# Expert loop of a hybrid decoder trunk: the down product of one expert moved behind the gate and up products of the next

## The reference

```python
def hier_moe(h, ...):            # top-1 of 4 groups, then top-2 of its 8 experts
    ...
    for e in range(N_EXPERTS):   # 32
        y = (jax.nn.silu(t @ w_gate[e]) * (t @ w_up[e])) @ w_down[e]
        out = out + combine[:, e:e + 1] * y
```

## Time and profile before

| | |
|---|---|
| median of 3 runs | 908.18 us (905.06 to 909.02) |
| the profiled execution | 908.32 us, its span 906.6 us |
| TensorE matmul busy | 829.3 us, 91% of the span |
| TensorE weight load busy | 573.5 us, 63% |
| VectorE / ScalarE / GpSimd busy | 331.0 / 200.2 / 153.5 us |
| moved by DMA | 265.19 MB |

### The profile page before, as it was taken

The page is one execution under the profiler, slowest core; times in us unless marked ns, Lnnn a source line. Parts: engine busy times, 40 slices in busy tenths (PEclk is TensorE's granted clock), DMA queues, the critical chain, the costliest instruction groups (busy, mean ns, idle before and its releaser), DMA issues.

```text
span 906.6 us, 15450 instructions
## 1 busy us (share of the span) xinstructions
PE 829.3 (91%) x5319; PEld 573.5 (63%) x5320; DVE 331.0 (37%) x608; ACT 200.2 (22%) x295; POOL 153.5 (17%) x241
## 2 busy tenths in 40 slices
PE   7999999999999999998998999999999999878850
PEld 6888878888888888895554555455545555434420
DVE  3799996841555246257111101111011111010107
ACT  4633435141542224141000000000000000000003
POOL 4231801000230000010311122112211122211100
PEclk9999999999999999999999999999999999999985
DMA  8693321833234938558999999999999999999966
GB/s 263 130 195 97 115 71 21 173 94 97 90 94 146 418 130 309 226 207 330 399 417 422 419 421 422 424 423 425 423 422 425 421 422 426 422 423 426 420 249 241
DMA packets 71744, 265.19 MB, mean 292 GB/s; under 512 B 29526, under 2 KB 30550, under 8 KB 54516
## 3 DMA queue, kind: packets, MB, share of 16 engines
q1 hardware_dynamic: 65428, 254.10, 73.9%
q0 software_dynamic: 6128, 10.45, 3.1%
q10 hardware_dynamic: 144, 0.02, 0.0%
HBM read 256.59 MB, written 16.52 MB: 301 GB/s over the span
## 4 chain that ended last, share of the span: by engine, by line
PE 75%; SPq 10%; DMA 6%; DVE 5%; issue 2%; ACT 1%; POOL 0%; DVEq 0%; POOLq 0%; ACTq 0%
PE ps L1070 35%; PE ps L465 19%; PE ps L481 10%; SPq L448 7%; DMA slot_x<-in_exp_w_gate 5%; PE ps L1055 2%; SPq L446 2%; PE ps L1047 1%; PE ps L471 1%; DVE pair L709 1%; DVE pair L704 1%; DMA ssm<-choice_rows 1%; DVE hl L754 1%; PE ps L1215 1%; PE ps L591 1%
## 5 line engine op out<-in xcount | busy, mean ns | idle before, releaser
L704 DVE TENSOR_TENSOR pair<-pair,ps 128x256 f32<-128x256 f32 x32 | 13.5, 421 | 338.7 <-PE ps L465 338.7
L1070 PE MATMUL ps<-h_hi,w_hi 128*128 128x512 f32 x280 | 109.2, 390 | 0.0
L1070 PE MATMUL ps<-h_hi,w_lo 128*128 128x512 f32 x280 | 109.0, 389 | 0.0
L1070 PE MATMUL ps<-h_lo,w_hi 128*128 128x512 f32 x280 | 108.9, 389 | 0.0
L1497 DVE TENSOR_TENSOR w_lo<-raw,w_hi 128x1024 fp32r<-128x1024 f32 x56 | 71.7, 1283 | 99.7 <-ACT w_hi L1301 99.0
L1301 ACT CAST w_hi<-raw 128x1024 fp32r<-128x1024 f32 x59 | 61.8, 1050 | 189.4 <-PE ps L1070 189.4
L465 PE MATMUL ps<-ssm,pair 128*64 128x256 f32 x832 | 94.5, 384 | 4.9 <-DMA ssm<-in_exp_w_gate 4.1
L465 PEld LDWEIGHTS ps<-ssm,pair 128*64 128x64 f32 x832 | 61.0, 139 | 42.5 <-issue 15.1
L768 ACT COPY late<-ps 128x512 f32<-128x512 f32 x35 | 20.5, 586 | 300.2 <-PE ps L481 300.2
L852 POOL DMA_INDIRECT choice_rows<-late,put_now x35 | 35.6, 1017 | 295.4 <-ACT late L768 245.8
L1070 PEld LDWEIGHTS ps<-h_hi,w_lo 128*128 128x128 f32 x280 | 52.5, 188 | 11.0
(11 more groups left out here) (334 smaller groups left out, 1217.2 us busy)
## 6 DMA issues: line engine op xcount, KB each, us to landing
ssm<-in_exp_w_gate SPq DMA_DIRECT2D x16, 2048.0 KB, 25.9
raw<-in_w_in SPq DMA_DIRECT2D x40, 512.0 KB, 4.0
au<-in_exp_w_up SPq DMA_DIRECT2D x8, 2048.0 KB, 28.7
ssm<-in_exp_w_up SPq DMA_DIRECT2D x8, 2048.0 KB, 24.9
ssm<-in_exp_w_down SPq DMA_DIRECT2D x8, 2048.0 KB, 25.2
hl<-in_exp_w_down SPq DMA_DIRECT2D x8, 2048.0 KB, 28.6
slot_x<-in_exp_w_gate SPq DMA_DIRECT2D x8, 2048.0 KB, 32.1
raw<-in_exp_w_down SPq DMA_DIRECT2D x8, 2048.0 KB, 31.2
```

What stands on the lines that cost most here:

```text
L704: nc.vector.tensor_tensor(act_cols, silu_cols, up_now, ALU.mult).then_inc(act_ready, 1)
L1070: t = nc.tensor.matmul(bank, lhs, rhs, start=k == 0 and n == 0, stop=k == 2 * count - 1 and n == 2)
```

## The change

TensorE no longer runs expert e's down product in e's own turn. Its order in a turn is now: gate of e; the transposes of the product of e - 1; up of e; all four transposes of the rows of e + 1; down of e - 1; the second block of e - 1 if it has one. Expert 0 is as before, turn 1 has no down product in it besides, and expert 31's transposes and down product come after the loop.

The other loops follow: VectorE runs product(e), the gain for e + 1, the second block of e - 1, and then the copy for the down product of e. ScalarE runs silu of e and then the result of e - 1. GpSimd scatters the results one turn later. SyncE loads gate and up of expert e and then down of expert e - 1. The product of a second block has a place of its own (`act2_`), as `act_` is in use then.

```diff
--- before.py
+++ after.py
@@ -272,6 +272,7 @@
         place0, place1 = (a[:, 0:NT * CAP].rearrange("p (i s) -> p i s", i=NT) for a in (pair[:, 512:768], late))
         silu, act_ = pair[:, 1024:1280], pair[:, 1280:1536]
         actT = pair[:, 1536:1792].rearrange("p (j n) -> p j n", j=2)
+        act2_ = pair[:, 1792:2048]
         res = [late[:, W * b:W * (b + 1)] for b in range(2)]
         res2 = late[:, 2 * W:3 * W]
 
@@ -421,7 +422,7 @@
         turned = ps[:, B_XT].rearrange("p (j h t) -> p j h t", j=4, h=2)
         at_bank = ps[:, B_AT, 0:256].rearrange("p (j n) -> p j n", j=2)
         up_now, silu_cols = (a.rearrange("p (c j) -> p j c", j=2) for a in (ps[:, B_UP, 0:F // 2], silu))
-        act_cols = act_.rearrange("p (j c) -> p j c", j=2)
+        act_cols, act2_cols = (a.rearrange("p (j c) -> p j c", j=2) for a in (act_, act2_))
         rows0 = pair[:, 1024:1536]
         turned0 = ps[:, B_AT].rearrange("p (j h t) -> p j h t", j=4, h=2)
         HALF = F // 2
@@ -466,9 +467,9 @@
                                          w[:, k, HALF * h:HALF * (h + 1)], start=k == 0, stop=k == KD - 1)
             return t
 
-        def turn_act():
+        def turn_act(rows=act_):
             for j in range(2):
-                t = nc.tensor.transpose(at_bank[:, j], act_[:, P * j:P * (j + 1)], ident[:])
+                t = nc.tensor.transpose(at_bank[:, j], rows[:, P * j:P * (j + 1)], ident[:])
             return t
 
         def down(w_, bank, pe=None, rest=0):
@@ -522,19 +523,28 @@
             weights(sp, 3, "down", 3, ew_in[3]["down"])
             sp.wait_ge(second_known, 2)
 
-            def reload(e, w):
+            def reload(e, w, kinds):
 
                 flag, before = second_of(sp, e - SETS)
-                for kind in KINDS:
+                for kind in kinds:
 
                     sp.wait_ge(done[kind], e - SETS + 1)
                     sp.wait_ge(second_done, before * 3 + flag * DONE[kind] + 3)
                     sp.sem_inc(passed, 1)
                     weights(sp, w, kind, e, ew_in[w][kind])
 
-            with sp.Fori(1, NE // SETS) as i:
-                for w in range(SETS):
-                    reload(i * SETS + w, w)
+            def reloads(i):
+                for w in range(1, SETS):
+                    reload(i * SETS + w, w, KINDS[0:2])
+                    reload(i * SETS + w - 1, w - 1, KINDS[2:3])
+
+            reload(SETS, 0, KINDS[0:2])
+            with sp.Fori(1, NE // SETS - 1) as i:
+                reloads(i)
+                reload(i * SETS + SETS, 0, KINDS[0:2])
+                reload(i * SETS + SETS - 1, SETS - 1, KINDS[2:3])
+            reloads(NE // SETS - 1)
+            reload(NE - 1, SETS - 1, KINDS[2:3])
 
             def through(e):
                 flag, before = second_of(sp, e)
@@ -631,48 +641,56 @@
             def turn(e, w, nth, gathers, first):
 
                 after, half = (w + 1) % 2, w == SETS - 1
-                for kind, bank in (("gate", B_GATE), ("up", B_UP)):
-                    pe.wait_ge(ew_in[w][kind], nth * 16 + 16 * (PARTS if w == 2 else 1))
-                    if kind == "gate":
-                        pe.wait_ge(xgT_ready, e + 1)
-
-                    hidden(xgT, w, kind, bank, pe if half and kind == "up" else None, nth * 16 + 16).then_inc(done[kind], 1)
-
-
+                pe.wait_ge(ew_in[w]["gate"], nth * 16 + 16 * (PARTS if w == 2 else 1))
+                pe.wait_ge(xgT_ready, e + 1)
+                pe.wait_ge(silu_ready, e)
+                hidden(xgT, w, "gate", B_GATE).then_inc(done["gate"], 1)
+                if not first:
+                    pe.wait_ge(act_ready, e)
+                    turn_act().then_inc(at_full, 1)
+                pe.wait_ge(ew_in[w]["up"], nth * 16 + 16 * (PARTS if w == 2 else 1))
+                hidden(xgT, w, "up", B_UP, pe if half else None, nth * 16 + 16).then_inc(done["up"], 1)
                 pe.wait_ge(xg_in[after], gathers * 16)
-                turn_x(pe, xg[after], 0, 2)
-                pe.wait_ge(act_ready, e + 1)
-                turn_act().then_inc(at_full, 1)
-                turn_x(pe, xg[after], 2, 4).then_inc(xt_full, 1)
+                turn_x(pe, xg[after]).then_inc(xt_full, 1)
+                if not first:
+                    back(e - 1, (w - 1) % SETS, nth * 16 if w == 0 else nth * 16 + 16, 1)
+
+            def back(e, w, loads, ahead):
+                half = w == SETS - 1
                 pe.wait_ge(actT_ready, e + 1)
-                pe.wait_ge(ew_in[w]["down"], nth * 16 + 16)
-                if not first:
+                pe.wait_ge(ew_in[w]["down"], loads)
+                if not isinstance(e, int) or e > 1:
                     pe.wait_ge(res_ready, e - 1)
-                down(w, B_RES[w % 2], pe if half else None, nth * 16 + 16).then_inc(done["down"], 1)
-                second_block(e, w)
-
-            def second_block(e, w):
+                down(w, B_RES[w % 2], pe if half else None, loads).then_inc(done["down"], 1)
+                second_block(e, w, ahead)
+
+            def second_block(e, w, ahead):
                 flag, before = second_of(pe, e)
                 with pe.If(flag > 0):
 
                     pe.wait_ge(xg2_in, before * 16 + 16)
-                    pe.wait_ge(xgT_ready, e + 2)
+                    pe.wait_ge(xgT_ready, e + 2 + ahead)
+                    if ahead:
+                        pe.wait_ge(act_ready, e + 2)
                     turn_x(pe, xg2).then_inc(xt2_full, 1)
                     pe.wait_ge(xgT2_ready, before + 1)
                     hidden(xgT2, w, "gate", B_GATE).then_inc(second_done, 1)
                     hidden(xgT2, w, "up", B_UP).then_inc(second_done, 1)
                     pe.wait_ge(act2_ready, before + 1)
-                    turn_act().then_inc(at2_full, 1)
+                    turn_act(act2_).then_inc(at2_full, 1)
                     pe.wait_ge(actT2_ready, before + 1)
                     pe.wait_ge(res2_ready, before + 1)
                     down(w, B_RES2).then_inc(second_done, 1)
 
-            second_block(0, 0)
+            second_block(0, 0, 0)
             for w in range(1, SETS):
                 turn(w, w, 0, (w + 1) // 2, w == 1)
             with pe.Fori(1, NE // SETS) as i:
                 for w in range(SETS):
                     turn(i * SETS + w, w, i, i * 2 + (w + 1) // 2, False)
+            pe.wait_ge(act_ready, NE)
+            turn_act().then_inc(at_full, 1)
+            back(NE - 1, SETS - 1, NE // SETS * 16, 0)
 
             def over(o_, first):
                 pe.wait_ge(ov_xg_in, o_ * 16 + 16)
@@ -696,19 +714,24 @@
             each_over(pe, over)
 
         def experts_vector(v):
-            def turn(e, first):
+            def product(e):
                 v.wait_ge(silu_ready, e + 1)
                 v.wait_ge(done["up"], e + 1)
-                if not first:
+                if not isinstance(e, int) or e > 0:
                     v.wait_ge(at_full, e)
                 nc.vector.tensor_tensor(act_cols, silu_cols, up_now, ALU.mult).then_inc(act_ready, 1)
 
+            def turned_act(e):
                 v.wait_ge(at_full, e + 1)
-                if not first:
+                if not isinstance(e, int) or e > 0:
                     v.wait_ge(done["down"], e)
                 nc.vector.tensor_copy(actT, at_bank).then_inc(actT_ready, 1)
-                v.wait_ge(xt_full, e + 2)
+
+            def turned_rows(e):
+                v.wait_ge(xt_full, e + 1)
                 gain(xgT, turned).then_inc(xgT_ready, 1)
+
+            def second_block(e):
                 flag, before = second_of(v, e)
                 with v.If(flag > 0):
 
@@ -716,13 +739,24 @@
                     gain(xgT2, turned).then_inc(xgT2_ready, 1)
                     v.wait_ge(silu2_ready, before + 1)
                     v.wait_ge(second_done, before * 3 + 3 + DONE["up"])
-                    nc.vector.tensor_tensor(act_cols, silu_cols, up_now, ALU.mult).then_inc(act2_ready, 1)
+                    nc.vector.tensor_tensor(act2_cols, silu_cols, up_now, ALU.mult).then_inc(act2_ready, 1)
                     v.wait_ge(at2_full, before + 1)
+                    v.wait_ge(done["down"], e + 1)
                     nc.vector.tensor_copy(actT, at_bank).then_inc(actT2_ready, 1)
 
-            turn(0, True)
-            with v.Fori(1, NE) as e:
-                turn(e, False)
+            product(0)
+            turned_act(0)
+            turned_rows(1)
+            second_block(0)
+            product(1)
+            turned_rows(2)
+            turned_act(1)
+            with v.Fori(2, NE) as e:
+                product(e)
+                turned_rows(e + 1)
+                second_block(e - 1)
+                turned_act(e)
+            second_block(NE - 1)
 
             def over(o_, first):
                 v.wait_ge(ov_pe, o_ * OV_PE + OV_XT)
@@ -767,17 +801,18 @@
                     act.wait_ge(stored, stored_n)
                 nc.scalar.copy(dst, ps[:, bank]).then_inc(ready, 1)
 
```

(53 more changed lines are left out.)

## The result

| | before | after |
|---|---|---|
| median of 20 runs each | 907.86 us | 910.53 us |
| lowest to highest | 905.06 to 909.95 | 908.34 to 913.45 |
| ratio, 95% interval | | 1.0034 (1.0024 to 1.0044) |
| the profiled execution, its span | 908.32, 906.6 | 913.45, 911.4 |

The change costs 2.7 us by the medians, 3.1 by the ratio.

What follows compares the result with a forecast made beforehand. The prediction took the loop to be bound by its 192 MB of transfers. It summed 908.32 + 1.5 (start) + 0.5 (pinch) + 1.1 (tail) = 911.4, less 0.1, to 911.3 us; range 907.3 to 915.0.

Steps and rivals of the forecast that it cites:

- The bound: Main loop: transfers of 192 MB set the pace, 15.8 us an expert where TensorE needs 12.05.
- Rival A: Main loop: TensorE sets the pace after all, so its saved waits give 897.7 us; chance 0.04.
- TensorE's waits, worth 0: Turns of the loop: 0.33 us saved a turn, 10 us in 31 turns, becomes waiting for loads; worth 0.
- Start of the queue, 1.5 us: SyncE's queue behind up 4: nothing issued for 3.56 us, as down 4 now follows up 5; costs 1.5 us, bounds 0 and 3.3.
- The pinch at gate 15, 0.5 us: Reload of gate 15, behind second blocks of experts 10 and 11: queue nearest to dry; costs 0.5 us, bounds 0 and 2.4.
- Rival C: Gate of 15: the queue runs dry there; with the full gap at the start 915.0 us; chance 0.15.
- The tail, 1.1 us: After the last loads: second down product behind down 30's landing costs 1.1 us, bounds -0.2 and 2.8.
- Rival D: Ahead of down 30: TensorE idles 2.8 us and the clock falls; price 1.7 us, giving 913.0; chance 0.13.
- The range: Whole kernel: 907.3 to 915.0 us, the low end using 0.9 us by which runs of one kernel differ.

Runs made afterwards that it cites:

- kernel with both ends mended: Changed kernel with down 4 reloaded right behind up 4 again, and the last turn (down 30 ahead of gate 31) as before: 906.4 us, ratio 0.9977.
- the transposes: 11 identity transposes on TensorE ahead of down 0, added to the changed kernel (ratio 1.0027), to it with start and last turn as before (0.9984), to the kernel before (0.9993).

## Why the prediction came out right, point by point

- *The bound.* Shown from two sides: GB/s in the stretches didn't move, and halving the bytes took 23 us off the kernel before and turned the change's loss of 3 into a gain of 11. Rival A described the halved kernel, at its price of 10.5.
- *TensorE's waits, worth 0.* Right in that 10 us saved became 10 us of waiting. The kernel with both ends mended, which has the new turns and no other advantage that was looked for, is 2.1 us under the kernel before, and 0.8 us when both have the transposes. So the 0 was too high by up to 2 us. How much of it is real, and where it comes from, isn't shown.
- *Start of the queue, 1.5 us (0 to 3.3).* The mechanism is right in place and kind; undone, redone in the old kernel, and visible in the share. By the ratios it was sized too small: 2.5 us (1.5 to 3.5) in the kernel before, 4.2 and 3.7 in the changed one (1.0034 to 0.9988, and 1.0018 to 0.9977; with their intervals 2.2 to 5.4). In the traces without a fall of the clock ahead of down 0 it is nearer: the changed kernel's third load landed at 447.5 and those of the kernel before at 446.3 and 445.8, 1.2 and 1.7 us earlier, and at the end 1.8 us are left. What the ratios have beyond that isn't shown; a candidate is the fall of the clock, by which gate 1 is late while the queue stands empty, and which the bound of 3.3 left out.
- *The pinch at gate 15, 0.5 us.* In the changed kernel it came to nothing. Gate of 15 was issued at 595.68 (worked out: 597.1) and landed 14.0 us later, with a share of 1.00 from 590 to 600 us. The last row is of the kernel with both edits and the transposes:

```profile
595.68 0.33 SPq L449 DMA_DIRECT2D slot_x<-in_exp_w_gate  x1
slot_x<-in_exp_w_gate SPq DMA_DIRECT2D x1, 2048.0 KB, 14.0
...
590.00:600.00 10.00, 8.96 (x76) 5.03 (x74) 0.85 (x2) 0.39 (x1) 1.20 (x2) 1.00 0.94 376
```

  Rival C is out for the changed kernel. The last load ahead of gate 15 was down of 13, not up of 14 as the working names it, in the place that the working took; it landed at 604.8, so the lead was 9.1 us and not 4.7. TensorE was earlier than worked out, since the wait of 2.00 us and the slow gate and up behind it aren't in its trace, and the loads were later, since the gap at the start had held them back. In the three changed kernels with the start mended the pinch is there: shares of 0.97, 0.96 and 0.94 from 590 to 600 us, 0.3 to 0.7 us of transfers missing, near the 0.5 taken.
- *The tail, 1.1 us.* Down 31 starts 4.55 us after down 30 (worked out: 4.65), and the pair with the transposes gives 1.2. Taken out, it gives 1.0 to 1.5, with 0.4 of that outside the span, which I hadn't in the sum.
- *Rival D*, the clock ahead of down 30: seen in one execution of a variant at 1.7 us, not in the changed kernel's own trace, where the wait was 1.74 as well and the product took 3.65.
- *The range.* The 0.9 us by which runs of one kernel differ was read too small: the three runs of the table before lie 4.0 us apart, its 20 runs 4.9.

So the mechanism and both places of the loss were right, and that the total, 911.3 against 910.5, came so close is in part luck: by the ratios a start too small by 1 to 2.7 us and a missed 0.4 stand against a pinch of 0.5 that wasn't and a gain of up to 2 in the turns that I had at 0.

## What to carry to other kernels

When transfers set the pace, reordering products changes the time only through the order in which places come free: write down, for the first and the last two experts, which load waits for which product, and which products stand behind the last landing. Here the middle of the loop lost nothing and its two ends did, so filling and draining the software pipeline in the old order is worth a try. And a queue that has just been started has no stock: the one missing issue at 436 us was still seen in the last landings, 430 us later.

## What the runs showed of the hardware that I had not expected

- A load of 2048 KB into an empty queue takes 7.5 to 7.9 us from issue to landing, against 5.26 us a load in a full one.
- Whether the clock falls after a wait of under 2 us varies between executions of like kernels: ahead of down 0, behind a wait of 1.47 or 1.48 us in each of the nine kernels without the transposes, it fell in six traces (down 0 took 4.88 to 6.22 us) and not in three (3.65). Ahead of down 30 waits of 1.74 and 1.81 us went with 3.65 and 5.35 us.
- The device time outside the span is 1.7 us in some of the kernels and 2.1 in others, the same in every run of one kernel. Those with the last turn written out have 1.7, as does the kernel before. The cause is open.
- Still open as well: why the kernel with both ends mended is up to 0.2% faster than the kernel before.
